# Banded attention layer in three fp32r products of split operands, rests on GpSimd, and a new order at the head of each MLP

## The chip, the cores and the metric

The kernel runs on 1 core of one Trainium2 chip. Time is device microseconds of that core; the lower the better. The engines are TensorE (PE; its weight loads are shown as PEld), VectorE (DVE), ScalarE (ACT), GpSimd (POOL) and SyncE (SP, which here only issues transfers). Each has its own queue of instructions that runs in order, and they meet at semaphores.

## What is computed

One inference step of a trunk with 4 layers over 384 tokens (128 context, 256 latent) of width 1024. The token mixers are differential attention (layers 0 and 3), RWKV-7 time mixing (layer 1) and windowed grouped-query attention with a sink (layer 2). A squared-ReLU MLP follows each mixer. What the change touches:

```python
def adaln(x, shift, scale):
    return rms_norm(x) * (1 + scale) + shift
def squared_relu_mlp(h, w1, w2):                       # every layer, D_FF = 4096
    return jnp.square(jax.nn.relu(h @ w1)) @ w2
# layer 2, swa_context / swa_latent
q, k, v = split(h @ wqkv)                              # 16 query heads, 4 key/value heads, 64 wide
q, k = rms_norm(q), rms_norm(k)                        # latent tokens: also rotary
pr = softmax(concat([s_ctx, s_local, sink]))           # local keys within 128 of the query
out = (pr @ v) @ wo
x = x + gate * out
```

## The kernel before

Activations lie transposed: `xT` and `hT` are 8 tiles (`KT`) of 128 features by 384 tokens (`TOK`). Weights come in slabs of 1024 x 256 (1 MB) into 4 slots (`slab`); SP issues their loads in the order in which the phases use them, each when the slab four places earlier has been used.

**MLP, L587 to L768, one per layer.** Both operands of each product are split in a high part (rounded to fp32r) and a rest, and three fp32r products (high x high, high x rest, rest x high) take the place of one fp32 product. Weights: ACT makes the high part of a slab (`hi`, L675), DVE the rest (`lo`, L729), in two buffers `w[:, r % 2]`. The input: DVE normalises (`norm_dve`: a product with `rstd`, L414, then scale and shift for the two token groups, L420, two instructions for each tile), ACT copies each tile to `h[:, 0]` (L706), POOL takes the rest (L715). PE does for each slab r and its halves j = 0, 1 the 24 matmuls over k (L633). At the head of the MLP the order is: ACT: `hi(0, 0)`, then `norm_std` (Ln L389, Exp L392, waits for the sum of squares), then the 8 copies; DVE: `lo(0, 0)`, then `norm_dve`; PE: slab 0, half 0, which waits for the rest of tile k at each k.

**The banded layer, `swa`, L1263 to L1625.** Its products are plain fp32 matmuls on `hT` and the slabs. Head: ACT `norm_std`, DVE `norm_dve`, PE the two key tiles (`pe_project`, L1330), the three value tiles (`pe_values`, L1339), with head norms between them (`pe_sum`, `act_root`, `dve_norm`, `pe_partner`). Then a loop of slots s = 0 to 31. Query tile n (2 to 9) is projected in the three slots 3n' to 3n'+2 (thirds of 2, 3 and 3 tiles of k). A slot holds further, for attention units of a head pair and 128 queries: the scores of unit s-5 (PE), its maximum (`dve_max`) and exponentials (`act_exp`), the scaling (`dve_scale`) and turning (`pe_turn`) of unit s-6, and the copy (`act_turned`), product with v (`pe_out`) and copy (`act_out`) of unit s-7. In the first slot of a triple PE must have the accumulator of the last tile emptied by `act_raw` (L1416); ACT does that after the slot before. In slots 24 to 30 (`FILL`) PE takes pieces of the output projection (`pe_wo`, L1404) of three of its 8 column tiles; the rest follows behind the loop, with `residual` on DVE (L438) and the squares for the next norm on ACT (L376), summed by PE (L380). POOL does nothing in this layer.

An fp32 matmul has two records in the trace, an fp32r one has one.

## Time and profile before

| | us |
|---|---|
| Median of 3 runs | 2681.22 (2681.07 to 2684.25) |
| The profiled execution | 2681.02 |
| Its span in the trace | 2679.2 |
| PE busy | 2469.8 (92%) |
| DVE, ACT, POOL busy | 1115.5, 890.5, 313.2 |
| Banded layer, from about | 1600.6 to 1799.4 |
| Head of an MLP (end of the layer before to the end of the first slab's products) | 25 of each MLP |

A line of a timeline is: start, duration, engine, line, operation, output <- inputs, shape, count, and in brackets the idle time before it and who ended it. Merged lines of several instructions carry the span from the first start to the last end. Durations of single instructions contain a fixed part, so those that follow one another overlap.

### The profile page before, as it was taken

Reading aid. Unit: us, or ns where it says so; the run is one execution under the profiler, and the core shown is the slowest. Engines: PE = TensorE matmul, PEld = TensorE weight load, DVE = VectorE, ACT = ScalarE, POOL = GpSimd, SP = SyncE. Lnnn points to the kernel's source line nnn. Section 1 sums busy time; section 2 is a strip of 40 time slices with the busy share of each in tenths; the row PEclk is TensorE's granted clock in tenths of the full one; section 3 lists DMA queues with packets and bytes.
Section 4 is the critical chain, followed back from the end, with each engine's and each line's share of the span. In section 5 each row is a group of like instructions: output and inputs, shape, how many; then the busy total and the mean of one; then the engine's idle time right before and its main releaser. Section 6 shows DMA issues by size and latency. Waiting matters only on the chain. (4 is left out here: it accounts for less than half of the span.)

```text
span 2679.2 us, 51680 instructions
## 1 busy us (share of the span) xinstructions
PE 2469.8 (92%) x21864; PEld 1979.4 (74%) x21864; DVE 1115.5 (42%) x2039; ACT 890.5 (33%) x1643; POOL 313.2 (12%) x307
## 2 busy tenths in 40 slices
PE   4999889997998888889899999989999999889999
PEld 2566579996676777776699985448999765559998
DVE  2244253333414566562433334534333334434444
ACT  1344233333113344341332323523333244423332
POOL 0000021100012334330210100002111000011111
PEclk8999989999999999999899999999999999989999
DMA  8533265664121000001566641125656212124331
GB/s 274 176 111 126 82 202 188 196 202 132 63 95 38 9 13 8 9 9 49 173 192 201 194 138 48 52 78 190 206 194 195 95 63 79 56 88 134 128 128 57
DMA packets 310245, 312.74 MB, mean 117 GB/s; under 512 B 14306, under 2 KB 308012, under 8 KB 309932
## 3 DMA queue, kind: packets, MB, share of 16 engines
q1 hardware_dynamic: 302784, 304.09, 35.5%
q10 hardware_dynamic: 7276, 5.95, 0.7%
q8 instruction: 145, 2.38, 0.4%
q14 instruction: 40, 0.33, 0.0%
HBM read 305.55 MB, written 4.46 MB: 116 GB/s over the span
## 5 line engine op out<-in xcount | busy, mean ns | idle before, releaser
L633 PE MATMUL psum<-parts 128*128 128x384 f32 x6144 | 1116.1, 340 | 42.2 <-POOL parts L715 42.2
L633 PEld LDWEIGHTS psum<-parts 128*128 128x128 f32 x6144 | 1072.8, 190 | 89.3 <-issue 45.0
L729 DVE TENSOR_TENSOR parts<-slab,parts 128x2048 fp32r<-128x2048 f32 x128 | 293.4, 2293 | 210.7 <-ACT parts L675 210.7
L675 ACT ACTIVATE parts<-slab 128x2048 fp32r<-128x2048 f32 x128 | 244.8, 1913 | 376.8 <-PE psum L633 368.7
L438 DVE SCALAR_TENSOR_TENSOR xT<-psum,mod,xT 128x128 f32<-128x128 f32 x320 | 118.1, 413 | 407.4 <-PE psum L633 280.4
L721 POOL TENSOR_TENSOR parts<-room_mlp,parts 128x384 fp32r<-128x384 f32 x128 | 129.8, 1014 | 877.2 <-DVE room_mlp L739 877.2
L917 PE MATMUL psum<-hT,slab 128*128 128x384 f32 x512 | 185.1, 506 | 10.3 <-DVE hT L420 8.8
L739 DVE TENSOR_TENSOR room_mlp<-hT 128x384 f32<-128x384 f32 x128 | 71.4, 558 | 244.6 <-ACT hT L680 244.6
L680 ACT ACTIVATE hT<-psum 128x384 f32<-128x384 f32 x128 | 62.9, 491 | 325.9 <-PE psum L633 325.9
L917 PEld LDWEIGHTS psum<-hT,slab 128*128 128x128 f32 x512 | 94.4, 194 | 81.2 <-issue 23.6
L715 POOL TENSOR_TENSOR parts<-hT,parts 128x384 fp32r<-128x384 f32 x32 | 31.8, 999 | 1009.3 <-ACT parts L706 1009.3
L929 PE MATMUL psum<-slab,hT 128*128 128x256 f32 x384 | 91.2, 387 | 7.2 <-ACT room L1020 7.0
L929 PEld LDWEIGHTS psum<-slab,hT 128*128 128x128 f32 x384 | 70.3, 190 | 29.2 <-issue 13.6
L1000 PE MATMUL psum<-room,slab 128*128 128x384 f32 x256 | 89.1, 502 | 0.0
L1077 DVE SCALAR_TENSOR_TENSOR room<-room,small 128x384 f32<-128x384 f32 x32 | 19.8, 619 | 160.7 <-ACT room L1030 160.7
L1992 PE MATMUL psum<-room 64*64 64x64 f32 x1920 | 72.2, 223 | 11.7 <-DVE room L2338 9.5
L2234 POOL TENSOR_TENSOR room<-room,const 128x384 f32<-128x384 f32 x64 | 65.8, 1045 | 123.8 <-PE psum L1992 123.8
L376 ACT ACTIVATE hT<-xT 128x384 f32<-128x384 f32 x56 | 29.2, 522 | 150.9 <-DVE xT L438 144.8
L1992 PEld LDWEIGHTS psum<-room 64*64 64x64 f32 x1920 | 63.1, 136 | 21.8 <-DVE room L2338 16.4
L2338 DVE TENSOR_TENSOR room<-psum,room 128x384 f32<-128x384 f32 x64 | 35.2, 550 | 104.5 <-PE psum L2011 104.1
L268 PE MATMUL psum<-ada_slab,cond_pad 128*32 128x256 f32 x1152 | 77.1, 385 | 0.0
L1000 PEld LDWEIGHTS psum<-room,slab 128*128 128x128 f32 x256 | 49.3, 196 | 35.3 <-issue 5.1
(271 smaller groups left out, 3099.7 us busy)
## 6 DMA issues: line engine op xcount, KB each, us to landing
slab<-in_mlp_w SPq DMA_DIRECT2D x128, 1024.0 KB, 5.3
ada_slab<-in_ada_w SPq DMA_DIRECT2D x96, 1024.0 KB, 7.5
slab<-in_da_wqkv SPq DMA_DIRECT2D x24, 1024.0 KB, 5.6
slab<-in_rwkv_wrkv SPq DMA_DIRECT2D x12, 1024.0 KB, 5.3
slab<-in_da_wo SPq DMA_DIRECT2D x8, 1024.0 KB, 5.2
slab<-in_swa_wqkv SPq DMA_DIRECT2D x6, 1024.0 KB, 5.0
slab<-in_rwkv_wo SPq DMA_DIRECT2D x4, 1024.0 KB, 5.6
slab<-in_swa_wo SPq DMA_DIRECT2D x4, 1024.0 KB, 5.4
```

The lines of the kernel that those rows point to most:

```text
L268: mm = nc.tensor.matmul(psum[strip:strip + STRIP, 6, 0:SLAB], cond_pad[:, k, CONDAT - 2 * s:CONDAT - 2 * s + STRIP], ada_slab[:, s % ADA_S ...
L438: ins = nc.vector.scalar_tensor_tensor(x, acc[:, t], gate, x, ALU.mult, ALU.add)
L633: mm = nc.tensor.matmul(out, x(a), y(b), start=first and n == 0, stop=last and n == 2)
L675: nc.scalar.activation(w[:, r % 2, 0], slab[:, g % SLOTS], ACT.Copy).then_inc(sem("hi_ready"), 1)
L721: nc.gpsimd.tensor_tensor(hid[:, 1, n], square[:, n % 4], hid[:, 0, n].bitcast(F32), ALU.subtract)\
L729: nc.vector.tensor_tensor(w[:, r % 2, 1], slab[:, (start + r) % SLOTS], w[:, r % 2, 0].bitcast(F32), ALU.subtract).then_inc(split_ready, 1)
L739: nc.vector.tensor_tensor(square[:, n % 4], hT[:, n], hT[:, n], ALU.mult)\
L917: mm = nc.tensor.matmul(bank(PROJ, TOK), slab[:, u % SLOTS, kk, at:at + P], hT[:, kk], start=kk == 0, stop=kk == KT - 1)
L929: mm = nc.tensor.matmul(bank(PROJ, SLAB), hT[:, kk, t * P:(t + 1) * P], slab[:, u % SLOTS, kk], start=kk == 0, stop=kk == KT - 1)
L1000: mm = nc.tensor.matmul(bank(OUT_BANKS[g % 4], TOK), slab[:, (wo_start + u) % SLOTS, kk, half * P:(half + 1) * P], o[:, kk], start=kk == 0 ...
L1992: mm = nc.tensor.matmul(psum[head_half(1 - q_), G + 2 * z, i * CH:(i + 1) * CH], mask_at(st.j, lev)[q, z, i], T[q, z, i], start=True, stop ...
L2234: st.inc("lm_ready", nc.gpsimd.tensor_tensor(mask_at(st.j, lev)[:, z], LA[:, z], over(levels[:, z, lev - 1], 6), ALU.mult))
```

## The change

1. **Head of each MLP.** ACT: `norm_std` first, then `hi(0, 0)`; then ACT itself does scale and shift (two instructions for each tile, in place in `hT`), and the high copy of tile k-1 behind those of tile k. DVE: the products with `rstd` only, with `lo(0, 0)` behind the third. PE: for slab 0 first all products with the high part of h (both halves), which wait only for that copy, then those with its rest.
2. **Banded layer.** `h` and `w` (two buffers, high and rest) are new, in a part of the layer's room that is typed fp32r. Every projection, the values and the output projection are done as three fp32r products. High parts of 10 weight slabs and of 16 activation tiles: ACT. Rests of the activations: POOL. Rests of the slabs: POOL for slabs 0, 2, 3, 4, 5, 6 and 7, DVE for 1, 8 and 9. The key tiles are done product by product (`pe_keys`). In the slot loop ACT makes slabs 3, 4, 5, 6 and 7 at the end of slots 1, 7, 13, 19 and 25, and the high parts of the attention's output tiles at the end of slots 24, 25 and 28. `FILL` has other pieces. The layer's `o` lies in `hT`.

The diff, cut to its core (a line "..." marks what is left out):

```diff
@@ mlp, tensor
+                                    if r == 0:
+                                        for k in range(KT):
+                                            if j == 0:
+                                                pe.wait_ge(sem("h_hi"), base("h_split") + k + 1)
+                                            for a in range(2):
+                                                nc.tensor.matmul(bank(j, TOK), w[:, 0, a, k, j * P:(j + 1) * P], h[:, 0, k],
+                                                                 start=k == 0 and a == 0, stop=False)
+                                        continue
...
+                                if r == 0:
+                                    for j in range(2):
+                                        for k in range(KT):
+                                            if j == 0:
+                                                pe.wait_ge(sem("h_split"), base("h_split") + k + 1)
+                                            mm = nc.tensor.matmul(bank(j, TOK), w[:, 0, 0, k, j * P:(j + 1) * P], h[:, 1, k],
+                                                                  start=False, stop=k == KT - 1)
+                                        mm.then_inc(run_done, 1)
@@ mlp, scalar
+                        norm_std(act, layer)
                         hi(0, 0)
-                        norm_std(act, layer)
-                        for k in range(KT):
-                            act.wait_ge(sem("h_ready"), base("h_ready") + k + 1)
-                            nc.scalar.activation(h[:, 0, k], hT[:, k], ACT.Copy).then_inc(sem("h_hi"), 1)
+                        act.wait_ge(sem("mod_ready"), 2 * (layer + 1))
+                        for k in range(KT + 1):
+                            if k < KT:
+                                act.wait_ge(sem("xn_ready"), base("h_ready") + k + 1)
+                                for g, t in GROUPS:
+                                    ins = nc.scalar.activation(hT[:, k, t], hT[:, k, t], ACT.Identity,
+                                                               scale=mod[:, layer, 4 * KT + k, g:g + 1],
+                                                               bias=mod[:, layer, 3 * KT + k, g:g + 1])
+                                ins.then_inc(sem("h_ready"), 1)
+                            if k:
+                                act.wait_ge(sem("h_ready"), base("h_ready") + k)
+                                nc.scalar.activation(h[:, 0, k - 1], hT[:, k - 1], ACT.Copy).then_inc(sem("h_hi"), 1)
@@ mlp, vector
-                        lo(0, 0)
                         link = Link(dve, "dve_step")
-                        norm_dve(dve, link, layer, 1)
+                        dve.wait_ge(sem("std_ready"), base("sum_done"))
+                        for k in range(KT):
+                            if k == 3:
+                                lo(0, 0)
+                            nc.vector.tensor_tensor(hT[:, k], xT[:, k], rstd[:, :], ALU.mult).then_inc(sem("xn_ready"), 1)
@@ swa
+            h, w = f(2, KT, TOK), f(2, 2, KT, SLAB)
+            PRODUCTS = ((0, 0), (0, 1), (1, 0))
...
+            def pe_keys(pe):
+                for a, b in PRODUCTS:
+                    for e in range(KEY_TILES):
+                        for kk in range(KT):
+                            if (a, b, e, kk) == (0, 0, 0, 0):
+                                pe.wait_ge(sem("hi_ready"), sb + 1)
+                            if (a, e, kk) == (1, 0, 0):
+                                has_split(pe, 0)
+                            if a == 0 and e == 0:
+                                pe.wait_ge(sem("h_split" if b else "h_hi"), hb + kk + 1)
+                            mm = nc.tensor.matmul(bank(2 if e else PROJ, TOK), w[:, 0, a, kk, e * P:(e + 1) * P], h[:, b, kk],
...
@@ pe_wo
-                    wait(pe, "o_ready", TT * (kk + 1))
-                    mm = nc.tensor.matmul(bank(OUT_BANKS[g % 4], TOK), slab[:, (wo_start + u) % SLOTS, kk, j * P:(j + 1) * P],
-                                          o[:, kk], start=kk == 0, stop=kk == KT - 1)
+                    pe.wait_ge(sem("h_split"), hb + KT + kk + 1)
+                    for m, (a, b) in enumerate(PRODUCTS):
+                        mm = nc.tensor.matmul(bank(OUT_BANKS[g % 4], TOK), w[:, (WO + u) % 2, a, kk, j * P:(j + 1) * P],
...
-            FILL = {24: (0, (0, 1)), 25: (0, (2, 3)), 26: (0, (4,)), 27: (0, (5,)), 28: (0, (6,)),
-                    29: (1, (0, 1, 2, 3, 4, 5, 6)), 30: (2, (0, 1, 2, 3, 4, 5, 6))}
+            FILL = {25: ((0, (0, 1, 2)),), 26: ((0, (3, 4)),), 27: ((0, (5,)), (1, (0, 1))), 28: ((1, (2, 3, 4)),),
+                    29: ((0, (6,)), (1, (5, 6))), 30: ((2, (0, 1, 2, 3, 4, 5, 6)),)}
+            WO, UNITS = 6, 10
+            HI_AT = {1: 3, 7: 4, 13: 5, 19: 6, 25: 7}
+            OUT_AT = {24: (0, 1, 2, 3, 4), 25: (5,), 28: (6,)}
+
+            def act_w_hi(act, n):
+                has_slab(act, start + n)
+                if n >= 2:
+                    act.wait_ge(run_done, run_after[start + n - 2])
+                nc.scalar.activation(w[:, n % 2, 0], slab[:, (start + n) % SLOTS], ACT.Copy).then_inc(sem("hi_ready"), 1)
...
@@ swa, scalar
                     norm_std(act, layer)
+                    act_w_hi(act, 0)
+                    for kk in range(KT):
+                        act_h_hi(act, kk)
+                        if kk == 3:
+                            act_w_hi(act, 1)
                     act_raw(act, 0)
                     act_raw(act, 1)
                     act_root(act, 0)
                     act_values(act, 0)
+                    act_w_hi(act, 2)
                     act_root(act, 1)
...
+                        for kk in OUT_AT.get(s, ()):
+                            act_o_hi(act, kk)
+                        if s in HI_AT:
+                            act_w_hi(act, HI_AT[s])
+                    act_o_hi(act, KT - 1)
+                    act_w_hi(act, WO + 2)
+                    act_w_hi(act, WO + 3)
...
+                @block.gpsimd
+                def _(pool):
+                    w_lo(pool, nc.gpsimd, 0)
+                    for kk in range(KT):
+                        pool_lo(pool, kk, 0)
+                    w_lo(pool, nc.gpsimd, 2)
+                    for s in range(LAST + 1):
+                        for kk in OUT_AT.get(s, ()):
+                            pool_lo(pool, kk, 1)
+                        if s in HI_AT:
+                            w_lo(pool, nc.gpsimd, HI_AT[s])
+                    pool_lo(pool, KT - 1, 1)
@@ swa, vector
                     norm_dve(dve, link, layer, 0)
+                    w_lo(dve, nc.vector, 1)
...
-                    wo_dve(dve, wo, layer, OUT_BANKS)
+                    for g in range(KT):
+                        if g in (2, 4):
+                            w_lo(dve, nc.vector, WO + 1 + g // 2)
+                        dve.wait_ge(run_done, run_after[wo_start - 1] + g + 1)
+                        residual(layer, 0, g, bank(OUT_BANKS[g % 4], TOK)).then_inc(acc_taken, 1)
```

`w_lo(engine, ops, n)` waits for the high part of slab n and for the rest of slab n-1, and is one tensor_tensor over 128 x 2048; `pool_lo` is one over 128 x 384, behind the high copy of its tile.

## Rows read from the trace of the kernel before

**Rows 1.** Whole execution, from the page: busy us (share) x instructions.

```profile
PE 2469.8 (92%) x21864; PEld 1979.4 (74%) x21864; DVE 1115.5 (42%) x2039; ACT 890.5 (33%) x1643; POOL 313.2 (12%) x307
```

**Rows 2.** Stretches: us, busy PE, PEld, DVE, ACT, POOL, PEclk, DMA, GB/s.

```profile
1605.00:1630.00 25.00, 24.88 (x87) 17.42 (x88) 10.44 (x29) 4.88 (x10) 0.00 (x0) 0.91 0.13 43
...
1662.00:1734.00 72.00, 66.98 (x370) 35.01 (x370) 42.52 (x135) 38.28 (x125) 0.00 (x0) 1.00 0.11 32
```

**Rows 3.** Timeline of PE; min/median/max ns of one.

```profile
1578.09 4.43 PE L633 MATMUL psum<-parts 128*128 128x384 f32 x24
...
L633 PE MATMUL psum<-parts x6144: 331/334/690, 343.8 to 2669.9; 128*128 128x384 f32 x199
...
1785.04 5.32 PE L1404 MATMUL psum<-room,slab 128*128 128x384 f32 x16
...
L1404 PE MATMUL psum<-room,slab x128: 486/486/590, 1736.6 to 1795.7; 128*128 128x384 f32 x128
```

**Rows 4.** Timeline of layer 2's MLP head, all engines.

```profile
1796.01 3.39 PE L380 MATMUL psum<-hT,const 128*128 128x384 f32 x10
...
1799.75 1.91 ACT L675 ACTIVATE parts<-slab 128x2048 fp32r<-128x2048 f32 x1 [2.25 <-PEq L1487]
...
1801.70 2.29 DVE L729 TENSOR_TENSOR parts<-slab,parts 128x2048 fp32r<-128x2048 f32 x1 [4.74 <-ACT parts L675]
...
1802.16 0.52 ACT L392 ACTIVATE rstd<-rstd 128x384 f32<-128x384 f32 x1
...
1805.89 1.40 DVE L420 TENSOR_SCALAR hT<-hT,mod 128x128 f32<-128x128 f32 x2
...
1806.14 0.99 POOL L715 TENSOR_TENSOR parts<-hT,parts 128x384 fp32r<-128x384 f32 x1 [247.05 <-ACT parts L706]
...
1807.28 1.30 PE L633 MATMUL psum<-parts 128*128 128x384 f32 x3 [7.88 <-POOL parts L715]
...
1817.89 15.29 PE L633 MATMUL psum<-parts 128*128 128x384 f32 x78 [0.46 <-POOL parts L715]
...
1824.89 0.49 ACT L680 ACTIVATE hT<-psum 128x384 f32<-128x384 f32 x1 [3.63 <-PE psum L633]
```

**Rows 5.** ACT: scale and shift in layer 1's head; high copies of the MLPs.

```profile
662.35 8.14 ACT L2411 ACTIVATE room<-hT,mod 128x128 f32<-128x128 f32 x22 [0.69 <-DVE hT L414]
...
L706 ACT ACTIVATE parts<-hT x32: 522/523/525, 342.1 to 2404.6; 128x384 fp32r<-128x384 f32 x32
```

**Rows 6.** POOL's smallest operation (by shape); POOL and DVE together, layer 1.

```profile
L2431 POOL TENSOR_SCALAR room<-vecs 128x8 f32<-128x8 f32 x1 | 0.2, 197 | 0.0
...
1110.59 1.15 DVE L2288 TENSOR_TENSOR room<-room 128x384 f32<-128x384 f32 x1
...
1114.13 0.54 DVE L2297 TENSOR_TENSOR room<-room 128x384 f32<-128x384 f32 x1
...
1110.09 2.43 POOL L2213 TENSOR_TENSOR room<-room 128x384 f32<-128x384 f32 x2
```

**Rows 7.** Timeline of the banded layer's head.

```profile
1602.81 0.52 ACT L392 ACTIVATE rstd<-rstd 128x384 f32<-128x384 f32 x1
...
1610.59 1.26 DVE L420 TENSOR_SCALAR hT<-hT,mod 128x128 f32<-128x128 f32 x4
...
1605.12 12.91 PE L1330 MATMUL psum<-hT,slab 128*128 128x384 f32 x32 [4.58 <-DVE hT L420]
```

**Rows 8.** Timeline of its slot loop, one triple of slots.

```profile
1705.48 0.88 PE L1330 MATMUL psum<-hT,slab 128*128 128x384 f32 x2 [0.91 <-ACT room L1416]
...
1715.14 0.58 ACT L1437 ACTIVATE room<-psum,room 128x384 f32<-128x384 f32 x1 [3.62 <-DVE room L1475]
...
1716.50 0.16 DVE L1480 TENSOR_TENSOR room<-room 128x2 f32<-128x2 f32 x1 [1.39 <-ACT room L1439]
...
1719.90 0.91 PE L1330 MATMUL psum<-hT,slab 128*128 128x384 f32 x2 [0.81 <-ACT room L1416]
```

**Rows 9.** Timeline behind its slot loop.

```profile
1766.23 12.52 PE L1404 MATMUL psum<-room,slab 128*128 128x384 f32 x38 [0.38 <-ACT room L1450]
```

76 lines of the change are left out of this document (52 added, 24 removed).

## The prediction, made before the change was run

> **What bounds the kernel now.** I read the page first: PE is busy for 92% of the span [rows 1], so work taken from PE looks like time. A share over the whole span does not say that for one stage, so next come the stretches of the stages that the change touches, and last their timelines. In the MLPs, once they run, PE's matmuls follow one another without a gap, and each us of PE counts. Their heads are another matter: the layer before ends at 1799.40, PE's first MLP matmul starts at 1807.28, the last of the eight tiles k comes 7 x 1.77 later, and the second run of slab 0 ends only at 1824.9 [rows 4]. So 25.5 us pass for 48 matmuls that need 8.5. In the slot loop of the banded layer PE is busy for 67 of 72 us [rows 2], which looks like PE's bound too, but PE's idle time falls where the chain shows. Each triple of slots (1705.48 to 1719.90, 14.4 us) begins with PE waiting 0.8 to 0.9 for ACT's `act_raw`; ACT's exponentials had waited 3.62 for the maximum from DVE, and DVE's scaling 1.39 for them [rows 8]. Followed back, scores, maximum, exponentials, scaling, next maximum (DVE's queue holds them in this order), next exponentials, `act_raw` and the next triple's scores form a ring through ACT and DVE, in which PE has only short pieces. I take the loop to be bound by that ring.
>
> **Prices.** An fp32r matmul of 384 columns follows the last one after (4.43 - 0.33) / 23 = 0.178 us; an fp32 one is two records of (5.32 - 0.49) / 15 = 0.322, 0.644 in all [rows 3]. (4.43 and 5.32 span 24 and 16 records; 0.33 and 0.49 are what a single one takes.) Three fp32r products cost 0.534: a gain of 0.11 for each tile k, or 17%. The values have 256 columns: before, 16 records of 0.322 x 256/384 = 0.215 for a tile of tokens, 3.4 us; after, 24 records of between 0.119 (by columns) and 0.178 (if weight loads set the pace), 2.9 to 4.3. I take 3.6, since 24 loads are half as many again as 16, and call it a loss of 0.15 each.
>
> ACT makes the high part of a slab in 1.91, DVE the rest in 2.29, POOL the rest of one tile in 0.99 [rows 4]. POOL on 128 x 2048 isn't in the trace. From above: 0.99 x 2048/384 = 5.3. From below: POOL's smallest operation takes 0.20 [rows 6], and (0.99 - 0.20) x 2048/384 + 0.20 = 4.4. I take 4.5, nearer the lower end, as a fixed part certainly exists.
>
> What POOL does to DVE is in the rows. Two pairs of scale-and-shift on DVE take 1.26 with POOL idle, 0.63 a pair [rows 7]; one pair takes 1.40 when a POOL operation starts within it [rows 4]. A DVE operation with two inputs in SBUF takes 1.15 inside a run of POOL operations, a like one 0.54 just behind it [rows 6]. So either kind waits until POOL's operation ends, and POOL's 1 us operation costs DVE about 0.73. Whether a 4.5 us operation holds DVE for all of its time no row shows; nothing in these rows shows a release within an operation, so I take the whole of it, and a quarter of it as the lower bound. The Trainium skill, "SBUF — State Buffer", "SBUF: two separate sides", speaks against this change: VectorE and GpSimd share a port pair that is an "exclusive lock", held for a whole instruction, also against VectorE operations with two SBUF inputs. The rows of 1 us operations agree; by that rule the long operations block DVE in full. The Trainium skill, "GPSIMD Engine Reference", "Elementwise — side-by-side cycle accounting", gives 4497 ns for a two-input operation of 2048 fp32 elements; by it the sum would be the same.
>
> **MLP heads, four of them.** Time from the end of the layer before (1799.40). The block begins at 0.35. `norm_std` no longer waits for the high part of the slab: Ln and Exp (0.59 and 0.52) end at 1.46, the slab's high part 1.9 later, 3.3. DVE's first three products are done by then; its rest of the slab takes 3.3 to 5.6, so PE can start at 5.7 (before 7.9). Now ACT sets the pace. Scale and shift read from a tile: 22 such instructions in 8.14, with two of each four on a single column [rows 5], four in about 1.45; I split that as 0.89 for the two wide ones. With the copy at 0.43 behind its neighbours (0.52 alone) a tile costs ACT 1.32, against 1.77 before, when a POOL operation held DVE once in each tile. The copies end at 5.5 + 6 x 1.32 + 0.5 = 13.9. PE has then left the second half with the high part (16 matmuls) and both halves with the rest (16): 32 x 0.178 = 5.7, plus 0.4 for the last tile, plus about 1.0 for those at 1.2 GHz: in rows 4 three matmuls in 1.30 are 0.32 apart, so PE is at the lower of its two levels through this thin stretch, and the last tile and the first matmuls behind it still are. r = 0 ends at 21.1 instead of 25.1 (layer 0) to 25.5. POOL's rests keep up (1.0 for each tile, done at 14.9), slab 1 is split at 18.1, in time. DVE holds no 2-input work then that POOL could delay. Gain 4.0 each (2 to 5), as PE is without a gap from there on: **-16.0**.
>
> **Banded layer, head.** ACT's high part of slab 0 starts behind `norm_std`, 1603.3 to 1605.2. POOL then takes its rest until 1609.9, and DVE, with one or two of eight tiles normalised, stands. After that POOL's rest of each tile cuts into DVE as in the MLP heads. DVE's own work, 1603.4 to 1611.85 before [rows 7], ends 4.5 + 7.5 x 0.73 = 10 later, at 1621.9; the last high copy at 1622.4. PE then has 40 of 48 matmuls of the key tiles left: 7.1 us, plus 2.2 at the lower clock. That is what it lost here before: 25 us at a granted 0.91 [rows 2], beginning just as now behind an idle PE. Keys end at 1632.0, before at 1617.9 (32 records from 1605.12 for 12.9, [rows 7]): **+14.1** (by the same steps +9 if POOL holds DVE for a quarter only). Then POOL takes the rest of slab 2, started by ACT's high part right behind the first values: from 2.35 to 6.85 behind them. `dve_norm` of key tile 1 (two SBUF inputs, 0.6) comes at 7.5; PE, with one head sum and a value tile between, is there at 4.7: +2.8. Values: +0.4. Head: **+17.3**.
>
> **Slot loop.** Slots 0 to 5 have no ring yet: tile 2 is bound by PE and gives 0.9, a stretch of POOL's slab 3 costs 0.3: -0.6. In the six triples behind, PE's gain of 8 x 0.11 = 0.9 stays off the ring, all but the one piece between `act_raw` and the scores: -0.7 in all. ACT's 1.9 at the end of slots 7, 13 and 19 stands before the next copy and exponentials, of which about 0.9 is hidden in ACT's idle time; POOL's 4.5 begins with it and holds the scaling and with it the maximum of the slot after next. Laid over the triple of rows 8, ACT is done at 1718.5, POOL at 1723.0, the scaling ends at 1723.95, and the maximum 1.65 later than now: 3 x 1.65 = **+5.0** (0.9 each if POOL is no hindrance, 2.45 with POOL at 5.3). Slots 24 to 30: five rests of output tiles cut into DVE's ring, 5 x 0.73 = +3.7; slots 25 and 28 bring another slab (1.65) and two more tiles (0.8): +6.2; the last two slots hold 10 tiles k of output projection instead of 14, 10 x 0.534 against 14 x 0.644, -3.7, of which 0.9 returns in slots 27 and 28: **+3.4**.
>
> **Behind the loop.** 3 + 40 tiles k at 0.11 give -4.7; before, these ran from 1766.23 on with only 0.38 of waiting [rows 9]. The last output tile needs ACT's copy (0.52), POOL's rest (1.0) and two semaphores first: +1.7. Slabs 8 and 9 are split under PE's halves of 4.3: the first needs 1.9 + 2.3 behind run 1 and PE has 4.8 of work there. **-3.0**. DVE's residuals wait behind that, and nobody for them.
>
> The layer: 17.3 - 0.6 - 0.7 + 5.0 + 3.4 - 3.0 = +21.4. Kernel: 2681.0 + 21.4 - 16.0 = **2686.4** against the profiled execution's own 2681.02, which lies 0.2 under the median of 2681.22; I leave that out and say 2686.4.
>
> **Rivals.** (B) POOL's long operations don't hold DVE for their length. The head loses 4.5 + 2.8 less, the loop 3 x 0.75, slot 25 0.8: layer +11.0, kernel 2676. For it: the rows have POOL at 1 us only. Against: those show no release. (C) The slot loop is PE's, as its 67 of 72 us say. Then tiles 3 to 9 give 0.9 each, the waits are taken up by PE's shorter work, and the layer is +21.4 - 5 - 5 - 1 = +10.4 and with the fill's full gain of 2.3 about +6: 2671. For: the busy share. Against: the 0.8 us for `act_raw` in each triple. (D) The other side, dearer: POOL takes 5.3 on a slab. From 4.5 up each further 0.1 costs 0.1 six times (slabs 0, 2, 4, 5, 6, 7): +4.8, 2691. This case is slower by any reading, and the change stays so as long as a slab on POOL costs over about 4.5. (E) The MLP heads give 2 each, if ACT's scale and shift don't overlap (1.6 a tile) and PE stays at 1.2 GHz for longer: 2694.
>
> **How the numbers follow.** Forecast 2686.4, own range 2679 to 2694, chance 0.44; B 0.16; C 0.12; D 0.18; E 0.10. A difference under 0.2% (5.4 us) can't be told from none. The forecast lies on that bound: of its 0.44 0.23 count as slower, 0.19 as same, 0.02 as faster. B is same or faster in halves (0.08 each), C faster, D slower with 0.17 of 0.18, E slower. Faster 0.22, same 0.28, slower 0.50. The range takes in B, D and E and half of C: 2670 to 2699.
>
> **What would show it.** MLP heads: first high-part matmul about 5.7 behind the layer before, `L680`'s counterpart for run 1 at 21. Banded layer: one POOL operation of 4.4 to 5.3 from about 1605 (less 8 gained in two MLP heads) with DVE empty beside it, key tiles done 14 later than now relative to `norm_std`; in the loop, triples of 14.3 with two of three of 16. Wrong would be: triples of 13.5 (C), DVE working inside POOL's long operation (B), or a gap before slab 1 in the MLPs.

## The result and the profile after

| | before | after |
|---|---|---|
| median, us | 2681.15 | 2696.82 (2694.15 to 2700.3) |
| profiled execution, us | 2681.02 | 2695.33 |
| its span, us | 2679.2 | 2693.5 |

The changed kernel takes 1.0056 times as long as the one before (95% interval 1.0040 to 1.0072): slower, by 15.7 us. The forecast was +5.4 with a range of -11 to +18. The four medians of before that stand beside the runs in this text lie between 2681.15 and 2683.06, and its single runs between 2676.58 and 2686.07, so each ratio is taken against the runs of before that were made beside it.

First I cut both traces at the ends of the sums of squares that close each layer (the last L380 of each; for the last MLP at the start of the final transposes). This takes the whole kernel apart without a gap, in us:

| stage | before | after | difference |
|---|---|---|---|
| attention 0 | 335.95 | 336.36 | +0.4 |
| MLP 0 | 318.87 | 315.63 | -3.2 |
| recurrent layer 1 | 627.01 | 623.86 | -3.2 |
| MLP 1 | 318.72 | 315.26 | -3.5 |
| banded layer 2 | 198.85 | 229.11 | +30.3 |
| MLP 2 | 319.30 | 316.05 | -3.3 |
| attention 3 | 268.55 | 268.69 | +0.1 |
| MLP 3 | 284.12 | 280.75 | -3.4 |

Layer 1 has no changed instruction. It took either about 624 or about 627 to 628 in the ten further kernels too, in no relation to their code. A kernel's total thus carries 3 to 4 us that no edit made, and below I compare stages first and totals second.

The page of after still says that PE is busy for 91% of the span. Below it stands the longest group of PE's waits in the whole kernel, which is the start of the four MLP heads (us in total, times, longest). As in [rows 1], the page alone shows neither the loss nor the gain.

```profile
PE 2461.6 (91%) x22032; PEld 2005.8 (74%) x22032; DVE 1131.9 (42%) x1978; ACT 941.3 (35%) x1733; POOL 370.2 (14%) x330
...
PE psum L651 <- DVE parts L752: 23.3, 4, 5.8
```

**MLP heads.** The timeline of layer 0's MLP, whose layer before ends at 336.36 (start, length, engine, line, tile, count, idle time before it and its releaser); the pattern to hold beside [rows 4]:

```profile
342.17 1.95 PE L651 MATMUL psum<-parts 128*128 128x384 f32 x4 [5.81 <-DVE parts L752]
...
344.40 1.01 PE L651 MATMUL psum<-parts 128*128 128x384 f32 x2 [0.28 <-ACT parts L729]
...
349.57 5.80 PE L651 MATMUL psum<-parts 128*128 128x384 f32 x20 [0.28 <-ACT parts L729]
...
355.21 2.93 PE L667 MATMUL psum<-parts 128*128 128x384 f32 x16
```

PE starts 5.81 behind the layer's end and then gets a tile every 1.29 us (344.40 to 349.57 are four of them). The first slab's two halves end at 358.0, 21.6 behind (PE's next matmul starts then).

**Banded layer, head.** The layer before ends at 1591.11. All engines, to be read against [rows 7]:

```profile
1595.78 4.59 POOL L1473 TENSOR_TENSOR split<-slab,split 128x2048 fp32r<-128x2048 f32 x1 [46.12 <-ACT split L1466]
1595.92 5.54 DVE L420 TENSOR_SCALAR hT<-hT,mod 128x128 f32<-128x128 f32 x2
1596.26 0.66 PE L1362 MATMUL psum<-split 128*128 128x384 f32 x1 [5.15 <-ACT split L1478]
1602.08 0.69 PE L1362 MATMUL psum<-split 128*128 128x384 f32 x1 [5.16 <-ACT split L1478]
...
1610.89 10.50 PE L1362 MATMUL psum<-split 128*128 128x384 f32 x42 [1.73 <-ACT split L1478]
...
1621.59 3.32 PE L1385 MATMUL psum<-split 128*128 128x256 f32 x24
...
1628.19 3.96 DVE L1535 SCALAR_TENSOR_TENSOR room<-room,small 128x384 f32<-128x384 f32 x1 [4.04 <-ACT room L1505]
...
1632.21 0.70 PE L1400 MATMUL psum<-room,const 128*128 128x256 f32 x2 [3.36 <-DVE room L1535]
```

GpSimd's 128x2048 rest and DVE's scale and shift start together, and DVE's pair, 0.63 before, lasts 5.54. PE has its first tile at 1596.26 and its second 5.8 us later. The same happens at 1628.19: a product of 0.6 us takes 3.96, and PE idles 3.36 for it.

**Banded layer, slots.** Around the end of the slot in which ACT cuts a slab:

```profile
1695.11 1.92 ACT L1466 ACTIVATE split<-slab 128x2048 fp32r<-128x2048 f32 x1
...
1697.10 4.53 POOL L1473 TENSOR_TENSOR split<-slab,split 128x2048 fp32r<-128x2048 f32 x1 [27.77 <-ACT split L1466]
...
1697.78 0.88 PE L1433 MATMUL psum<-room 128*64 128x128 f32 x12 [2.20 <-ACT room L1524]
1698.55 3.10 DVE L1559 TENSOR_TENSOR room<-room 128x2 f32<-128x2 f32 x1 [1.59 <-ACT room L1518]
...
1700.59 1.48 PE L1395 MATMUL psum<-room,const 128*128 128x384 f32 x2
...
1703.12 0.43 DVE L1551 TENSOR_TENSOR psum<-psum,const 128x256 f32<-128x256 f32 x1 [0.76 <-PE psum L1411]
```

ACT's copy puts off the turned copy for which PE waits 2.20. GpSimd's rest follows, and a DVE operation on 128x2 elements, 0.16 us elsewhere, is held for 3.10. PE's two head sums take 1.48, against 0.81 in an undisturbed slot. The last line says which of the two delays counts here: DVE has done the held sum and the scaling behind it and then idles 0.76 for PE's scores (L1411), which come late because PE waited 2.20 and ran the groups behind the wait more slowly. The stretches of slots 6 to 23, 24 to 30 and behind the loop (length, busy time of PE, its weight loads, DVE, ACT, POOL, then PE's granted clock, DMA):

```profile
1652.00:1747.00 95.00, 79.61 (x481) 53.49 (x482) 60.53 (x164) 51.83 (x153) 13.60 (x3) 0.93 0.12 40
1747.00:1793.00 46.00, 32.79 (x187) 22.82 (x187) 22.10 (x43) 17.99 (x50) 12.98 (x9) 0.85 0.04 14
1793.00:1820.00 27.00, 27.00 (x143) 24.71 (x142) 10.16 (x18) 7.58 (x10) 0.00 (x0) 1.00 0.44 135
```

The granted clock, 1.00 in the like stretches of before ([rows 2] shows the middle one of them), is 0.93 and 0.85. In slots 24 to 30:

```profile
1751.80 2.17 ACT L1484 ACTIVATE split<-hT 128x384 fp32r<-128x384 f32 x5
...
1752.05 0.67 PE L1400 MATMUL psum<-room,const 128*128 128x256 f32 x2 [2.27 <-ACT hT L1529]
...
1761.84 4.50 DVE L1554 TENSOR_TENSOR room<-room 128x2 f32<-128x2 f32 x1
...
1762.48 0.88 PE L1433 MATMUL psum<-room 128*64 128x128 f32 x12 [2.56 <-ACT room L1524]
...
1771.52 2.26 PE L1451 MATMUL psum<-split 128*128 128x384 f32 x6 [4.30 <-ACT room L1518]
...
1792.37 10.19 PE L1451 MATMUL psum<-split 128*128 128x384 f32 x57 [2.00 <-POOL split L1489]
```

Five copies of output tiles in one go on ACT, a slab, and waits of PE of 2.0 to 4.3, one behind the other. In slot 26 GpSimd's rest of slab 7 also falls on the maximum itself: its last step, on 128x2 elements, takes 4.50, and ACT's exponentials wait 3.94 for it. Here is where the layer's 30 us are, and where mine stood (head and slots 0 to 5 together are 47.0 of before):

| part of the layer | before | after | difference | forecast |
|---|---|---|---|---|
| head | 30.3 | 44.9 | +14.6 | +17.3 |
| slots 0 to 5 | 16.7 | 15.9 | -0.8 | -0.6 |
| slots 6 to 23 | 87.4 | 94.9 | +7.5 | +4.3 |
| slots 24 to 30 | 31.3 | 45.6 | +14.3 | +5.1 |
| behind the loop | 33.2 | 27.9 | -5.3 | -4.7 |

(The 1.7 that I gave to the last output tile is moved to slots 24 to 30 here, since PE waits for it before its first matmul behind the loop.)

### The profile page after: what moved, and what is told of

It reads as the page before. It is cut to its first block and busy times, and to the rows that moved or that the text cites. A ratio compares the mean times of both kernels' runs of the same rounds, so it can differ in the third digit from the quotient of the medians.

```text
span 2693.5 us, 52164 instructions
## 1 busy us (share of the span) xinstructions
PE 2461.6 (91%) x22032; PEld 2005.8 (74%) x22032; DVE 1131.9 (42%) x1978; ACT 941.3 (35%) x1733; POOL 370.2 (14%) x330
## 5 line engine op out<-in xcount | busy, mean ns | idle before, releaser
L633 PE MATMUL psum<-parts 128*128 128x384 f32 x5376 | 958.4, 336 | 0.0
L633 PEld LDWEIGHTS psum<-parts 128*128 128x128 f32 x5376 | 929.2, 188 | 32.0 <-DVE xT L438 11.1
L943 PE MATMUL psum<-hT,slab 128*128 128x384 f32 x512 | 185.4, 507 | 10.1 <-DVE hT L420 8.8
L738 POOL TENSOR_TENSOR parts<-hT,parts 128x384 fp32r<-128x384 f32 x32 | 37.9, 1213 | 774.6 <-ACT parts L729 774.6
L651 PE MATMUL psum<-parts 128*128 128x384 f32 x512 | 116.4, 382 | 28.9 <-DVE parts L752 23.3
L651 PEld LDWEIGHTS psum<-parts 128*128 128x128 f32 x512 | 100.2, 215 | 43.3 <-issue 25.6
L955 PEld LDWEIGHTS psum<-slab,hT 128*128 128x128 f32 x384 | 70.3, 190 | 29.2 <-issue 13.6
L2103 PEld LDWEIGHTS psum<-room 64*64 64x64 f32 x1920 | 62.9, 136 | 22.4 <-DVE room L2449 16.5
```

Source lines behind the costliest of these rows:

```text
L633: mm = nc.tensor.matmul(out, x(a), y(b), start=first and n == 0, stop=last and n == 2)
L651: nc.tensor.matmul(bank(j, TOK), w[:, 0, a, k, j * P:(j + 1) * P], h[:, 0, k], start=k == 0 and a == 0, stop=False)
L943: mm = nc.tensor.matmul(bank(PROJ, TOK), slab[:, u % SLOTS, kk, at:at + P], hT[:, kk], start=kk == 0, stop=kk == KT - 1)
L955: mm = nc.tensor.matmul(bank(PROJ, SLAB), hT[:, kk, t * P:(t + 1) * P], slab[:, u % SLOTS, kk], start=kk == 0, stop=kk == KT - 1)
L2103: mm = nc.tensor.matmul(psum[head_half(1 - q_), G + 2 * z, i * CH:(i + 1) * CH], mask_at(st.j, lev)[q, z, i], T[q, z, i], start=True, stop ...
```

## The experiments

My theory after the result: GpSimd holds VectorE for the length of each of its instructions, and the slot loop is a ring through ScalarE and VectorE; the 9 us that the forecast missed lie in the placing of the new work in that ring. The rivals: the operations of GpSimd cost little and the work on ScalarE all; or one of the two parts of the change does not do what it says. The table holds the banded layer of every kernel with a changed one, cut at the same places (head and slots 0 to 5 in one column); each section refers to it. The last column is the slot loop from PE's partner product of slot 7 (`pe_partner`) to that of slot 25, which leaves out slot 6.

| kernel | to slot 6 | slots 6 to 23 | 24 to 30 | behind | layer | slots 7 to 24 |
|---|---|---|---|---|---|---|
| before | 47.0 | 87.4 | 31.3 | 33.2 | 198.9 | 87.8 |
| after | 60.8 | 94.9 | 45.6 | 27.9 | 229.1 | 95.5 |
| e2 | 63.2 | 96.2 | 45.6 | 27.9 | 232.8 | 95.2 |
| e3 | 53.7 | 94.9 | 44.0 | 29.4 | 221.9 | 95.5 |
| e4 | 60.8 | 94.9 | 42.5 | 27.9 | 226.0 | 95.4 |
| e5 | 56.1 | 96.2 | 44.1 | 29.4 | 225.7 | 95.2 |
| e6 | 63.3 | 97.3 | 46.4 | 29.4 | 236.3 | 96.3 |
| e7 | 53.6 | 88.6 | 39.6 | 29.4 | 211.3 | 89.2 |
| e10 | 47.0 | 87.9 | 38.3 | 27.9 | 201.1 | 88.4 |

Three differences in this table stand where no edit is. The head takes 2.5 longer in e2 and e6 than in after; slot 6 takes 1.5 longer in e2, e5 and e6; and behind the loop the same 57 matmuls take 10.2 at a granted clock of 1.00 in after and e10, but 11.7 at about 0.85 in e3 and e7 (29.4 in the table, as in e5 and e6). Instructions and waits are the same in each case and PE's clock is not, so what an edit does in the loop is read from the last column.

**Each part alone (e1, e2).** e1 is the kernel before with the diff's hunks in the MLP; e2 the kernel before with the hunks in the banded layer.

> Part 1 of the change alone; the banded layer is that of the kernel before. Theory: in the trace of the changed kernel each MLP is 3.2 to 3.5 us shorter than before (315.3 to 315.6 against 318.7 to 318.9 for the first three), 13.3 in all, and the RWKV layer, whose code is the same, 3.2 shorter (623.9 against 627.0). If both belong to the new MLP head, this run takes 2664 to 2668. Rival: the RWKV layer's 3.2 is a whim of one execution; then 2667 to 2670. Second rival: the heads' gain needs nothing of the banded layer and is 4.0 each as predicted: 2665 with an RWKV layer of 627.

Measured: 2666.39, ratio 0.9945 (0.9929 to 0.9962). The MLPs took 315.69, 315.19, 315.80 and 280.70, 3.2 to 3.5 less than before each; the banded layer 198.85, as before to the hundredth. Layer 1 took 624.0, but it took 623.5 in e2 too, whose MLP heads are those of before: its 3.2 don't come with the heads.

> Part 2 alone; the MLPs are those of the kernel before. Theory: the banded layer costs 30.3 us more wherever it stands (229.1 against 198.9): 2711, and layer 2's MLP is no longer than before. If the 3.2 of the RWKV layer came with the MLP heads, it is 627 here. Rival: part of the 30 us is paid by what follows the new MLP head (POOL or ACT busier there): then less than 2708.

Measured: 2714.53, ratio 1.0125 (1.0108 to 1.0142), the layer 232.8. That is 3.7 more than the same code takes in after, though the waits up to PE's 3.36 for DVE's held product are the same. The stretch of seven us behind this wait, and the 24 matmuls of the last value tile, which took 3.22 in after; first e2, then after:

```profile
1638.00:1645.00 7.00, 6.75 (x33) 6.43 (x33) 2.56 (x8) 0.74 (x3) 0.00 (x0) 0.60 0.00 0
...
1638.91 5.30 PE L1359 MATMUL psum<-split 128*128 128x256 f32 x24
```

```profile
1632.00:1639.00 7.00, 6.68 (x40) 5.38 (x41) 2.43 (x8) 1.09 (x4) 0.00 (x0) 1.00 0.30 95
```

The granted clock is 0.60 in one execution, so mostly the lower of the two levels, 1.2 GHz, and 1.00 (2.4 GHz) in the other, behind the same idle time of PE. Another piece of the 3.7, 1.3, lies in slots 6 to 23, in slot 6. The two parts add up, -16.5 and +31.6 against 15.7 for both: the change is a gain and a loss in one diff. And a wait of PE costs its own length and at times more: behind the 3.36 it was 2.5 more in e2 and nothing in after.

**Slab rests on VectorE (e3).** In the loop one slot later, behind the maximum:

```diff
-  w_lo(pool, nc.gpsimd, 0)      # and slab 2; in the slots: HI_AT[s]
+  w_lo(dve, nc.vector, 0)       # and slab 2; in the slots: HI_AT[s - 1]
```

> The changed kernel with the rests of all slabs on DVE; in the slot loop one slot later, behind that slot's maximum. Theory (POOL's 4.5 us operation holds DVE for its whole length, in the head and at each slab of the loop): the head loses its 4.5 standstill and the 2.8 to 3.4 before the second key tile's partner: -7.3; in slots 7, 13, 19 a slab costs about 1.0 instead of 2.35, -4; slot 26 -1.5: 2684. Rival (the lateness is ACT's 1.9 us copy in front of the next exponentials, POOL is beside it): head -4.5 at most, loop unchanged or later by DVE's own 2.3 for each slab, 2692 to 2700.

Measured: 2688.39, ratio 1.0023 (1.0013 to 1.0033), the layer 7.2 shorter: the theory held for the head and fell for the loop. Of these, 7.1 lie ahead of slot 6 (1.6 are gained in slots 24 to 30 and 1.5 lost behind the loop, where the first 57 matmuls took 11.7 in place of 10.2): PE has its second tile of k 1.7 behind the first (1596.88, 1598.57), not 5.8, and its 3.36 for the partner is gone. In slots 6 to 23 nothing changed, 94.9. Two triples with a slab in them took 31.04 (1677.69 to 1708.73), with GpSimd 31.03 (1697.78 to 1728.81). ScalarE's copy and PE's wait for the turned copy behind it are still there:

```profile
1688.61 1.92 ACT L1466 ACTIVATE split<-slab 128x2048 fp32r<-128x2048 f32 x1
...
1690.56 2.29 DVE L1473 TENSOR_TENSOR split<-slab,split 128x2048 fp32r<-128x2048 f32 x1
...
1691.28 0.88 PE L1433 MATMUL psum<-room 128*64 128x128 f32 x12 [2.20 <-ACT room L1524]
```

I read this as: in the slots the copy costs and GpSimd nothing. That holds for this order of the copy, as e5 confirms; e6 showed that it doesn't hold for another. The hold also goes the other way: here GpSimd's two rests of the last tiles of k took 6.00 behind VectorE's two slab rests (in after 3.98 behind one), at about 1 each alone, and PE waits 1.32 for them.

**Column tile 1 out of slot 27 (e4).** Tile 1 writes PSUM bank 2, one of the two banks of scores, so its first matmul waits for the exponentials of the last scores. The change starts it in slot 27; before, it began in slot 29.

```diff
-  27: ((0, (5,)), (1, (0, 1))), 28: ((1, (2, 3, 4)),), 29: ((0, (6,)), (1, (5, 6)))
+  27: ((0, (5,)),), 28: ((1, (0, 1, 2, 3)),), 29: ((0, (6,)), (1, (4, 5, 6)))
```

> The changed kernel, with no piece of column tile 1 of the output projection in slot 27: it gets 4 tiles k in slot 28 and 3 in slot 29. Theory: in slot 27 PE stands 4.3 us (1767.2 to 1771.5) because column tile 1 goes to a bank of the scores and waits for the exponentials of unit 22, whose scores PE has only just done in this slot. Without that the stretch from slot 24 to the output tiles behind the loop is 4 to 5 us shorter (41 instead of 45.6), and PE keeps the higher clock in it for longer: 2691. Rival: the 4.3 are the ring's lateness (rests on POOL before DVE's scaling) that would come out anywhere: stretch within 1.5 us of 45.6, time 2695 to 2697.

Measured: 2694.67, ratio 1.0047 (1.0030 to 1.0064); the layer 3.1 shorter, all of it in slots 24 to 30 (42.5, where I had expected 41). The wait of 4.30 at 1771.52 is gone; PE waits 1.00 and 1.24 at other places for it, and twelve products of 128x128 behind it that took 1.55 take 0.88. The rival, a stretch of 44 or more, fell. That the total is nearer to the rival's comes from layer 1, which took 627.3 in this execution and 623.9 in that of after.

**GpSimd's rests in pieces (e5).** Eight operations of 128x256 in place of one of 128x2048:

```diff
-  ops.tensor_tensor(w[:, n % 2, 1], slab[...], w[:, n % 2, 0].bitcast(F32), ALU.subtract)
+  for c in range(8):  # kk = one tile of the eight
+      ops.tensor_tensor(w[:, n % 2, 1, kk], slab[..., kk], w[:, n % 2, 0, kk].bitcast(F32), ALU.subtract)
```

> The changed kernel, with each of GpSimd's seven slab rests cut into eight operations of 128x256 behind one another. If GpSimd holds VectorE only for the length of one of its own instructions (my theory), VectorE gets in between the pieces: the norm of key tile 1 (3.96 us in the changed kernel) comes down to 0.6 to 1.2 us, PE's wait of 3.36 us for it to under 1, and the banded head is 2 to 3 us shorter; the first rest, 4.59 us in one piece, may take 0.3 to 0.5 more. In the slots nothing moves if it is ScalarE's 1.92 us high copy at the slot's end that costs there (as the run with the rests on VectorE says: a pair of triples took 31.0 us with and without GpSimd); they gain 1.5 us each if it is the hold. Theory: 2694 (layer 226.5). Rival, the hold costs in the slots: 2689. Rival, the hold lasts across back-to-back GpSimd operations: no change, 2697.

Measured: 2692.34, ratio 1.0043 (1.0029 to 1.0057), the layer 3.4 shorter: 4.7 gained up to slot 6, 1.3 longer in slots 6 to 23, 1.5 gained up to slot 30 and 1.5 lost behind.

```profile
1626.82 0.86 DVE L1540 SCALAR_TENSOR_TENSOR room<-room,small 128x384 f32<-128x384 f32 x1 [4.04 <-ACT room L1510]
1627.73 0.70 PE L1400 MATMUL psum<-room,const 128*128 128x256 f32 x2 [0.25 <-DVE room L1540]
...
1648.42 1.48 PE L1395 MATMUL psum<-room,const 128*128 128x384 f32 x2
...
1662.14 5.53 POOL L1477 TENSOR_TENSOR split<-slab,split 128x256 fp32r<-128x256 f32 x8 [18.22 <-ACT split L1467]
```

The held product of 3.96 takes 0.86, PE's wait of 3.36 is 0.25. The eight pieces take 5.53 in all, 0.69 each, against 4.54 in one. So the hold lasts for one instruction of GpSimd; VectorE gets in between two of them, at 1.0 us more for GpSimd. In the slots the 128x2 sums are not held either, 0.16 each, and still slots 7 to 24 take 95.2, as in e2 and within 0.3 of after: with the copy at the slot's end GpSimd's hold costs this part of the loop nothing. The 1.3 in slots 6 to 23 aren't the pieces' doing: they lie in slot 6, ahead of the first slab, where the head sums take 1.48 at 1648.42 as in e2 (0.81 in after).

**High copies where ScalarE idles (e6).** From the end of slots 1, 7, 13, 19 and 25 to the next slot, ahead of its exponentials:

```diff
+  if s - 1 in HI_AT:
+      act_w_hi(act, HI_AT[s - 1])
   if a["scores"] is not None:
       act_exp(act, a["scores"])
...
-  if s in HI_AT:
-      act_w_hi(act, HI_AT[s])
```

> The changed kernel, with ScalarE's high copies of the five slabs cut in the slots moved from the end of a slot to a place in the next slot: behind its turned copy, before its exponentials, where ScalarE idles for 3.62 us. GpSimd's rests follow as before. Theory: in the slots it is the 1.92 us copy that costs, because the turned copy for which PE then waits 2.20 us stands behind it; in the gap it is free. Five events lose their 2.35 us or most of it: slots 6 to 23 fall from 94.9 to 88 to 90 us, the layer from 229.1 to 219 to 222, the kernel to 2687 to 2690. Rival, GpSimd's 4.5 us hold on VectorE costs as much wherever the copy stands: slots 6 to 23 stay at 94 to 96, kernel 2696 to 2698.

Measured: 2697.32, ratio 1.0056 (1.0036 to 1.0076): the theory fell, and the time is the one that the rival gave, the same as that of after (2696.82). The profiled execution is the slowest of the four (2704.24), and its layer is 7.2 longer. Of these, 2.5 lie in the head, 1.5 in slot 6 and 1.5 behind the loop, where the edit changes nothing (see under the table). Slots 7 to 24 take 96.3 against 95.5, slots 24 to 30 0.8 more. So the move gained nothing and lost little. The trace:

```profile
1700.84 1.93 ACT L1466 ACTIVATE split<-slab 128x2048 fp32r<-128x2048 f32 x1
...
1701.02 0.88 PE L1433 MATMUL psum<-room 128*64 128x128 f32 x12 [0.41 <-ACT room L1524]
...
1702.84 4.54 POOL L1473 TENSOR_TENSOR split<-slab,split 128x2048 fp32r<-128x2048 f32 x1 [26.88 <-ACT split L1466]
1703.59 3.81 DVE L1559 TENSOR_TENSOR room<-room 128x2 f32<-128x2 f32 x1 [1.59 <-ACT room L1518]
...
1777.83 2.26 PE L1451 MATMUL psum<-split 128*128 128x384 f32 x6 [7.17 <-ACT room L1518]
```

The copy does stand in ScalarE's idle time, and PE's wait of 2.20 is 0.41. But GpSimd's rest follows it, later in the triple than in after, and holds VectorE's sum of 128x2, and with it the scaling and the next maximum, for 3.81 in place of 3.10. Here VectorE does not idle behind the held sum: the next maximum follows the scaling at once, so the hold is now what the ring waits for. Two pairs of triples took 31.4 (1672.74 to 1704.15) and 32.6 (to 1736.79) with 31.0 in after, and the wait of slot 27 grew to 7.17.

**The three edits together (e7).**

> The three edits together on the changed kernel: slab rests on VectorE, high copies before the exponentials, and column tile 1 of the output projection kept out of slot 27. If they add up: 7.2 (measured for the first) and 3.1 (measured for the third) and 7 to 9 for the second off the layer's 229.1: 210 to 213 us, kernel 2677 to 2680, still 11 to 14 us behind the version with the MLP heads alone (2666.4), since the banded layer of before took 198.85. Rival, the edits take the same time away (VectorE's rests now compete with its maxima in the same slots): layer 217 or more, kernel 2685.

Measured: 2676.48, ratio 0.9978 (0.9968 to 0.9987): just faster than before. The layer took 211.25 and the time is half a us below the expected 2677 to 2680: the edits added up, to 17.9.

```profile
1687.77 1.93 ACT L1466 ACTIVATE split<-slab 128x2048 fp32r<-128x2048 f32 x1
...
1689.74 2.29 DVE L1473 TENSOR_TENSOR split<-slab,split 128x2048 fp32r<-128x2048 f32 x1 [0.81 <-ACT split L1466]
...
1691.09 0.79 PE L1375 MATMUL psum<-split 128*128 128x384 f32 x3 [1.46 <-ACT room L1495]
...
1648.00:1735.00 87.00, 73.08 (x476) 48.37 (x475) 57.88 (x165) 50.24 (x151) 0.00 (x0) 1.00 0.11 37
```

The copy is where it was in e6 and the rest runs on VectorE in 2.29. PE waits 1.46 for `act_raw` as at every triple's start, two triples take 29.4 (28.8 with no slab in them), and the granted clock over the loop is 1.00. Together e3, e5, e6 and e7 say what no one of them says. ScalarE's copy delays the next maximum by way of the turned copy, PE and the scores; GpSimd's hold delays it by way of VectorE's scaling. Both ways end at the same maximum, and either alone is enough to delay the ring. For slots 7 to 24: with both 95.5, without the hold 95.5 (e3) and 95.2 (e5), with the copy in the gap 96.3 (e6), without either 89.2, before 87.8. One reserve: in e6 the hold also begins 0.7 later, against the exponentials before it, than in after, so how dear the hold alone would be in its old place no run shows.

**PE's order in the MLP heads (e8).** In e1, PE idles 0.28 of every 1.29 us while the tiles arrive, and has 34 products left behind the last tile. e8 is e1 with

```diff
-  for j in range(2): for k in range(KT): high(j, k)     # then low(0, all), low(1, all)
+  for k in range(KT):
+      high(0, k)
+      if k >= 2: high(1, k - 2)
+      if k >= 3: low(0, k - 3)
+  # high(1, 6..7), low(0, 5..7), low(1, all)
```

> Part 1 alone (2666.4), with PE's order in the first slab of each MLP changed: while ScalarE makes the tiles, PE does both column halves of the slab's high products and the first half's low product, a few tiles behind, in place of the first half alone; at the end 17 products are left in place of 34. Theory: the head is bound by ScalarE's 1.29 us a tile, PE has 0.28 us idle of it at a clock that is low because PE is idle, and five products a tile fit at the full clock (0.89 us) and nearly at the half clock (1.45 us): the first slab ends 17 to 19 us behind the layer's end, not 21.6; four heads gain 3 to 4.5 each, kernel 2649 to 2655. Rival: the clock stays low for all 48 products (0.29 each, 13.9 us from 7.6 behind the end), 21.5 behind: no gain, 2666. Rival: in the other twelve passes bank 1 is asked for 3.4 us sooner, before the last residual has left it: 0.3 to 0.5 each, 4 to 6 us given back.

Measured: 2651.59, ratio 0.9889 (0.9871 to 0.9907). The MLPs took 311.90, 311.91, 311.90 and 277.31, 3.3 to 3.9 less than in e1. The layer before ends at 334.64:

```profile
350.38 2.07 PE L655 MATMUL psum<-parts 128*128 128x384 f32 x11
...
352.40 8.62 PE L633 MATMUL psum<-parts 128*128 128x384 f32 x48
...
340.00:348.00 8.00, 7.14 (x24) 5.47 (x25) 5.80 (x6) 8.00 (x20) 7.66 (x7) 0.66 0.83 262
348.00:353.00 5.00, 5.00 (x28) 4.74 (x29) 2.76 (x2) 3.54 (x5) 1.90 (x3) 1.00 0.02 5
```

The first slab ends 17.8 behind the layer's end. The granted clock is 0.66 while the tiles arrive and 1.00 behind them; in after it was 0.50 and 0.66:

```profile
342.00:350.00 8.00, 6.41 (x13) 3.43 (x14) 5.51 (x5) 8.00 (x20) 7.74 (x7) 0.50 0.82 262
350.00:356.00 6.00, 6.00 (x25) 6.00 (x25) 2.29 (x1) 1.74 (x1) 1.57 (x2) 0.66 0.08 21
```

So of the gain one part is products taken out of the row behind the last tile, and another that those left run at 0.18 and not at 0.29 us. PE was less idle, and its clock rose sooner. The rival with twelve late banks did not show: the passes behind the first start without a wait.

**The first slab's high part on VectorE (e9).** e8 with

```diff
-  hi(0, 0)                                              # ScalarE
+  nc.vector.tensor_copy(w[:, 0, 0], slab[:, start % SLOTS])   # VectorE, while ScalarE does Ln and Exp
```

and PE's products with the slab's rest two tiles later.

> The version with the MLP heads alone and interleaved (2651.6), with the high part of each MLP's first slab made by VectorE, which is idle until the norm's factor is there, in place of ScalarE (1.89 us there, ahead of its first scale and shift), and with PE starting on high by high products, the products with the slab's rest two tiles behind. Theory: ScalarE's row of eight tiles starts up to 1.9 us sooner, and PE's last product with it: 17.8 becomes 15.9 to 16.6 behind the layer's end, 1.2 to 1.9 a head, kernel 2644 to 2647. Rival: VectorE's copy of 128x2048 takes over 2 us, so that its first norm product is late by what ScalarE saves: no gain, 2651.6; above 3 us it is slower.

Measured: 2656.13, ratio 0.9903 (0.9887 to 0.9920), the MLPs 0.3 to 1.1 longer than in e8 (the intervals of the two ratios overlap, so the loss is read from the stages). The theory fell, and not by the rival's mechanism:

```profile
336.96 1.23 DVE L804 CAST parts<-slab 128x2048 fp32r<-128x2048 f32 x1 [2.83 <-PEq L1170]
...
339.51 2.28 DVE L774 TENSOR_TENSOR parts<-slab,parts 128x2048 fp32r<-128x2048 f32 x1
...
343.10 0.99 ACT L745 ACTIVATE hT<-hT,mod 128x128 f32<-128x128 f32 x2 [0.78 <-DVE hT L809]
...
344.55 2.94 PE L654 MATMUL psum<-parts 128*128 128x384 f32 x8 [1.50 <-ACT parts L751]
```

VectorE's copy took only 1.23 and ScalarE's row began sooner. But VectorE makes the rest of the slab behind three products of the norm, as in e8, and ScalarE, now ahead, stands 0.78 for tile 3; PE waits 1.50 for it. The last copy ends 13.5 behind the layer's end, in e8 13.6, and the first slab 18.7 against 17.8, since PE has more products left by then: its order holds them back for two tiles, and its granted clock while the tiles arrive is 0.50 (342 to 350), in e8 0.66. In e8 the head was bound by ScalarE and all but bound by VectorE.

**The output projection alone (e10).** On e8; keys, values and queries in fp32 as before, with the order of e7. The outputs take the place of queries already used, since the tile of the layer's input is read to the end.

> The interleaved heads (2651.6) with a banded layer of which only the output projection is three products of split operands: keys, values and queries in fp32 as before, high copies before the exponentials, rests of the slabs on VectorE, tile 1 out of slot 27. From the reordered version's stretches: behind the loop 3.8 to 5.3 less than before, slots 24 to 30 up to 8.3 more: layer 198.9 plus 3 to 5, kernel 2655 to 2657; the output projection alone does not pay. Rival: the 8.3 came with the queries' split tiles in the same slots and PE's low clock there; without them slots 24 to 30 cost 2 to 3 more and the layer gains 1 to 3, kernel 2649 to 2651.

Measured: 2657.20, ratio 0.9910 (0.9893 to 0.9926), the layer 201.1, 2.3 more than before's. Behind the loop 5.3 are gained, in slots 24 to 30 7.0 are lost:

```profile
1745.77 3.13 PE L1454 MATMUL psum<-split 128*128 128x384 f32 x12 [1.99 <-ACT room L1521]
```

The theory held, with a smaller loss than the 3 to 5 that I expected; the rival, that slots 24 to 30 are dear only because of the queries' split tiles, fell. So neither of the two halves of the banded part pays in any order that I ran: the output projection costs 2.3, and the projections 10.1 on top (211.25 against 201.11; 1.5 of it is PE's clock behind the loop). An order is left that I didn't run: tile 1 still starts in slot 28 here and waits 1.99 for the exponentials, and PE waits 2.00 more for the last rest before its matmuls behind the loop. Before, tile 1 started in slot 29 without a wait. Whether it would pay there again, with up to 2.0 of the 2.3 to win, is untested.

## Why the prediction was right or wrong, step by step

The direction was right (slower 0.50 was the largest chance), the time lay within the range, near its upper end, and the forecast was 10 us low. In the profiled execution the layer cost 8.9 more than the forecast and the MLP heads gave 2.6 less; layer 1, with no changed instruction, was 3.2 shorter and hid a part of that. That the time still lay within the range is partly luck: the range reached up to 2699 for rivals whose causes did not occur. By its steps:

**MLP heads, -16.0.** Mechanism right, size off: 3.2 to 3.5 each, 13.4 in all. The start (5.7 forecast, 5.81), the cadence (1.32, 1.29) and the end of the first slab (21.1, 21.6) are as worked out. The term that was short is the "about 1.0 for those at 1.2 GHz": the 16 products and the last tile behind ran in 5.80, 0.29 each [rows 3 has 0.178], at a granted clock of 0.50, then 0.66. In e8, with PE less idle, those behind the last tile run at 0.18. One sentence was wrong and cost nothing here: "DVE holds no 2-input work then that POOL could delay". VectorE's products with `rstd` have two inputs in SBUF; three before GpSimd starts took 1.50, the five beside its rests 5.67 (from 341.84). At 1.1 a tile that is just under ScalarE's 1.29, and e9 ran into it.

**Banded head, +17.3.** Measured +14.6. Right: GpSimd's 4.5 us (4.54 to 4.59 measured, bounds 4.4 and 5.3), the hold over its whole length, the 2.8 for the partner (3.36). e5 makes the hold more than a coincidence in time, by an experiment: the same work in eight instructions lets VectorE in. The rule of the Trainium skill, "SBUF — State Buffer", "SBUF: two separate sides", that whichever of the two engines starts first holds the shared ports for its whole instruction, agrees, down to 128x2 elements held for 3.10 and 3.81 us; and "GPSIMD Engine Reference", "Elementwise — side-by-side cycle accounting", with its 4497 ns agrees with 4.54 us. Two terms were too dear: keys were done at 1621.4, 30.3 behind the layer's end, for which I had 31.5; and the three value tiles with their head sums, PE's wait of 3.36 taken off, took 11.4 (1621.22 to 1635.98), 1.5 less than before (12.95, 1617.87 to 1630.82) and not 0.4 more, since 24 matmuls of 256 columns took 3.22 to 3.33, 0.13 each, and not 3.6.

**Slots 6 to 23, +4.3.** Measured +7.5, 2.5 for each of three slabs. The ring was right: a triple without a slab took 14.4 as in [rows 8], and PE's cheaper products gave nothing there, so rival C fell. The term that was too small is "3 x 1.65", and its mechanism was the wrong one of two: it charged GpSimd's hold and called ScalarE's 1.9 half hidden. In after it is the other way round. VectorE is done with what the hold delayed 0.76 before the scores come, so in slots 6 to 23 the hold costs nothing (e3, e5), and the copy at the slot's end costs 2.2 in the triples of slots 13 and 19 (16.6 against 14.4) and 3.5 in that of slot 7 (19.0 against 15.5 before). The hold becomes the limit only when the copy is out of the way (e6). What the step left out is PE's clock, 0.93 over the loop against 1.00 before and 1.00 in e7: behind the wait of 2.20 PE's groups take 1.24, 1.31 and 1.48 in place of 0.88, 0.79 and 0.81, and the scores stand behind them.

**Slots 24 to 30, +5.1.** Measured +14.3: the step that failed most, 9.2 too low, while the misses of the layer's other parts (-2.7, -0.2, +3.2, -0.6) cancel to -0.3. I had moved tile 1 to slot 27 and priced its products, but not the wait in front of them: the code stands in plain view, `if g in (1, 2): wait(pe, "exp_done", 3 * (N - 1))`, and I asked of each moved piece what it costs and not what its first instruction waits for. That is 3.1 (e4). Another 2.9 go away with the other two edits of e7 (42.5 to 39.6); one of the delays that they remove is the 4.50 for which GpSimd held the maximum. Of the 8.3 that are left, e10 shows 7.0 that come with the output projection in that order of pieces, 2.0 of them a wait for the exponentials in slot 28. I had taken "five rests of output tiles, 5 x 0.73" from VectorE's side alone; on ScalarE the five high copies run in one piece of 2.17 between two units' copies. How the rest of the 7.0 divides between the copies, GpSimd's rests and PE's clock (0.94 over the last 27 us of these slots in e10, 0.91 over all of them in e7) was not taken apart and stays open.

**Behind the loop, -3.0.** -5.3; for the 43 tiles alone I had -4.7; the 1.7 for the last output tile came as a wait of 2.00 in front.

**The rivals.** B (no hold) and C (PE's loop) are refuted by rows and runs. D's price, 5.3 for a slab, was wrong (4.5 measured), and E, two a head, was wrong (3.4). Their 2691 and 2694 lie nearer to the measured time than my forecast, by luck. None of my cases had the cause that decided, the waits of the pieces moved into the loop's last slots.

## What to carry to other kernels

An operand split for a faster matmul needs two more passes over it on other engines. They are free where those engines idle, as in an MLP in steady state, and cost more than the matmul gives where the stage is a ring through just these engines. Read which engine closes the ring before adding work to it, however busy PE is.

When two new delays reach the same point by different ways, taking away either one alone shows next to nothing. Try both before clearing one, and look which engine idles just before the point where they meet: it names the way that is not the limit. And before you give a difference to an edit, look whether it lies in a stretch that the edit changes.

In a stage that starts thin, give the engine that waits all products that its inputs already allow, of both halves: this gave 14.8 us here on top of e1, nearly as much as the 16.5 of e1, and brought the kernel to 2651.6, 1.1% under before. For every piece moved, read what its first instruction waits for.

## What the runs showed of the hardware

PE's granted clock fell behind some of PE's idle times of 2 to 5 us and not behind others: 0.60 and 1.00 behind the same 3.36 us of waiting, in two executions of the same instructions. It was 0.50 over a stretch in which PE had two products in each 1.29 us, and 0.66, then 1.00, with five (after and e8).

A GpSimd operation on 128x2048 (4.5 us) held VectorE instructions on 128x2 elements, 0.16 alone, for 3.10, 3.81 and 4.50; each ended with the GpSimd operation, to 0.02. One on 128x384 (0.62 alone) took 3.96 and ended 0.4 behind it. VectorE held GpSimd too: two rests of 128x384, 1.0 each alone, took 3.98 behind one VectorE subtraction of 128x2048 (after) and 6.00 behind two (e3). Eight pieces of 128x256 took 5.53 us against 4.54 for one of 128x2048, and let VectorE through between them.

VectorE copied 128x2048 from fp32 to fp32r in 1.23 us, against 1.89 to 1.93 on ScalarE and 2.29 for a subtraction of two such operands.
